# Nine norm statistics as two rounded passes, with the low parts of the squares on VectorE

## The chip, the cores and the metric

The kernel runs on one core of a Trainium2 chip. The metric is the device time of one execution in microseconds (us), as the median of several executions. A profile of one execution of the kernel before is at hand: its span is counted from the first to the last instruction, and all times of the trace are from the start of that span.

## The reference, cut to what matters

The model is a decoder of two layers. Each layer norms its input, projects it to queries, keys and values of three kinds of heads, mixes tokens, projects back, and runs a squared-ReLU MLP. Everything is float32. The change concerns the norms of the sparse-attention (dsa) and latent-attention (mla) queries and keys:

```
y = xf * rsqrt(mean(xf * xf, axis=-1) + RMS_EPS)        # rms_norm

q_d = rms_norm(heads(d_q, 4), dsa_q_norm)               # heads of 64
k_d = rms_norm(heads(d_k, 4), dsa_k_norm)
q_m = heads(rms_norm(m_cq, mla_q_latent_norm) @ mla_w_uq, 4)     # heads of 96
q_m = rms_norm(q_m, mla_q_norm)
k_m = rms_norm(concatenate([k_nope, k_rope]), mla_k_norm)
score = sum over 8 index heads of iw * relu(iq . ik), and the 128 largest keys of each query are kept
```

With 512 tokens, `min(256, L // 4)` keeps 128 keys for each query.

## The kernel before, in words

Activations lie with features on the 128 partitions and the 512 tokens in the free dimension. The mean square of a norm is a sum over partitions, so it is a matmul on TensorE: ScalarE writes the squares into `sqb` (two buffers in turn), TensorE multiplies them by `ones` or by the block matrix `blk`, and every output partition gets the sum. ScalarE then makes the factor from it with Ln and Exp (`factor`, `key_factor`) in `rsb`, and VectorE multiplies by the factor (`dsa_queries`, `dsa_keys`, `mla_queries`, `mla_keys`).

The weights come as a stream of units of 128x1024 floats. ScalarE makes a rounded high part of each unit in `wh` (type float32r), and the low part `wl = raw - wh` is a subtraction: by VectorE for units up to 10 (`low_part`), by GpSimd for later units of the input projection (`POOL_LOW`). A unit of the projection is 24 matmuls on float32r operands: high by low, high by high, low by high, for each of 8 blocks of inputs. The input projection has 24 units (`UNITS`, 0 to 23), in this order around the change: 8, 9 the dsa queries dq0 and dq1; 10, 11 the dsa keys dk0 and dk1; 12, 13 the GLA queries gq0 and gq1; 14, 15 the GLA keys gk0 and gk1; 16 to 19 the gates gg0 to gg3; 20 to 23 the GLA values.

Between the units TensorE runs small float32 matmuls in an order written out by hand: after unit 10 the statistic of mla query head 0 (`mqst0`) and of dq1 (`dqst1`), then the matmul of mla query head 1 (`mla_q(1)`); after unit 11 `mqst1`, `dkst0`, `mla_q(2)`; after unit 12 `mqst2`, `dkst1`, `mla_q(3)`; after unit 13 `mqst3`, the rotation `krot`, `mla_k(0)`; after unit 14 `mkst0` (two matmuls that add up in one bank) and `mla_k(1)`; after unit 15 `mkst1` and `mla_v(0)`.

Every engine has a queue of its own in program order, and they meet at semaphores. For unit u, ScalarE's loop waits for the unit's end, makes the high part of unit u+2 (`split`), and then does `tasks(u)`. VectorE's loop does `evacuations(u)` (it waits for the unit's end and takes the bank out of PSUM), then a number of selection steps (`per_slot`), then its own `tasks(u)`. A selection step finds the next eight largest scores of a block of 128 queries (MAX8) and marks them as taken (MATCH_REPLACE8) over a row of 512, 384 or 256; there are 48 in a layer. GpSimd's loop waits for the high part, makes the low part, and then scales decays (`scale_decay`) and turns queries (`turn_query`). `mla_queries(h)` is two VectorE instructions on operands in SBUF. In `factor`, the Exp of a statistic waits for `nrs_used` of the statistic two places earlier in `NORMS`, because there are two buffers `rsb`:

```python
act.wait_ge(*nrs_used.at(l, i - 2))
act.activation(rsb[0:rows, i % 2, cols], lnb[0:rows, cols], ACT.Exp, scale=-0.5)
```

NORMS runs: cqst, ckvst, dqst0, mqst0, dqst1, mqst1, dkst0, mqst2, dkst1, mqst3, mkst0, mkst1, and then nine of the later stages. So the factor of mqst1 waits until `mla_queries(0)` is done, that of mqst2 for `mla_queries(1)`, and that of mqst3 for `mla_queries(2)`.

Of the kernel before, what the change touches and what calls it, by code (L numbers as in the profile page):

```python
# [15 lines left out]
F32 = mybir.dt.float32  # L16
# [4 lines left out]
P = 128  # L21
T = 512
# [184 lines left out]
ACT_LINKS = 2  # L207


def build_trunk(nc, x_in, stream, params, consts, out):  # L210
    with ExitStack() as ctx:
# [36 lines left out]
        vm, _ = place("vm", [P, TB, H * DH])  # L248
        gated, _ = place("gated", [P, 2, T])
# [27 lines left out]
        ones, _ = place("ones", [P, P])  # L277
        low_rows, _ = place("low_rows", [P, P])
# [72 lines left out]
        nsq_ready = S("nsq_ready", N_NORM)  # L351
        nrs_ready = S("nrs_ready", N_NORM, start=1)
# [83 lines left out]
        def _(pool):  # L436
# [18 lines left out]
            for l in range(DEPTH):  # L455
# [30 lines left out]
                for u in POOL_LOW:  # L486
                    pool.wait_ge(*hi_ready.at(l, u + AHEAD))
                    pool.tensor_tensor(wl[:, u % 2], raw[:, u % 2], wh[:, u % 2], ALU.subtract)\  # L488
                        .then_inc(lo_ready.sem, 1)
                    if u == 9:  # L490
                        pool.wait_ge(const_loaded, 16)
                        scale_decay(0, 0)
                        scale_decay(0, 1)
                        turn_query(0, scaled.at(l, 1))
                    if u in (10, 11):
                        scale_decay(1, u - 10)
                        turn_query(u - 9, scaled.at(l, u - 8))
# [35 lines left out]
        def _(pe):  # L533
# [63 lines left out]
            for l in range(DEPTH):  # L597
# [30 lines left out]
                def mla_q_stat(h):  # L628
                    stat(l, f"mqst{h}", ones[0:QK, 0:QK], sq_of(f"mqst{h}")[0:QK], QK)
# [83 lines left out]
                pe.wait_ge(*rows_ready.at(0, 4))  # L713
# [10 lines left out]
                stat(l, "dqst1", blk, sq_of("dqst1"))  # L724
# [3 lines left out]
                stat(l, "dkst0", blk, sq_of("dkst0"))  # L728
# [3 lines left out]
                stat(l, "dkst1", blk, sq_of("dkst1"))  # L732
# [246 lines left out]
        def _(act):  # L979
# [47 lines left out]
            act.wait_ge(const_loaded, 16)  # L1027
            for l in range(DEPTH):
# [16 lines left out]

                def query_square(h):

                    square(f"mqst{h}", B[f"mq{h}"][0:QK, :], slice(0, QK), wait=B.filled(l, f"mq{h}"))
# [41 lines left out]
                def tasks(u):  # L1090
# [46 lines left out]
                    if u == 9:  # L1137
                        query_square(0)
                        factor("dqst0", DH)
                        square("dqst1", dqr[:, 1], wait=B.freed(l, "dq1"))  # L1140
                    if u == 10:
                        factor("mqst0", QK, QK)
                        query_square(1)
                        factor("dqst1", DH)
                        square("dkst0", dkn[:, 0], wait=B.freed(l, "dk0"))
                    if u == 11:
                        factor("mqst1", QK, QK)
                        query_square(2)
                        factor("dkst0", DH)
                        square("dkst1", dkn[:, 1], wait=B.freed(l, "dk1"))  # L1150
# [146 lines left out]
        def _(vec):  # L1297
# [8 lines left out]
            vec.memset(turn_rows[QK:P], 0.0).then_inc(rows_ready.sem, 1)  # L1306

# [40 lines left out]
            for l in range(DEPTH):  # L1348
# [155 lines left out]
                def tasks(u):  # L1504
# [25 lines left out]
                    if u == 9:  # L1530
                        mla_turn(0)
                        dsa_queries(0)
                    if u == 10:
                        mla_queries(0)
                        mla_turn(1)
                        dsa_queries(1)
                    if u == 11:
                        mla_queries(1)
                        mla_turn(2)
                        dsa_keys(0)  # L1540
                    if u == 12:
                        mla_queries(2)
                        mla_turn(3)
# [347 lines left out]
```

## Time and profile before

| | |
|---|---|
| median of 3 runs | 1248.28 us (1248.27 to 1248.38) |
| the profiled execution | 1248.1 us |
| its span | 1246.3 us, 17707 instructions |
| TensorE (PE) busy | 1236.8 us, 99% of the span |
| VectorE (DVE) busy | 753.1 us, 60% |
| ScalarE (ACT) busy | 527.2 us, 42% |
| GpSimd (POOL) busy | 227.5 us, 18% |
| granted TensorE clock | 1.000 |

Matmuls overlap in the records, so the duration of one is more than the distance from one start to the next; that distance is the price of a matmul in a full row. The shares are means over the whole span, in which the MLP takes by far the longest part; the change lies in a stretch of some 50 us in each of the two layers.

### The profile page before, as it was taken

The numbers are of one execution on the slowest core, as the hardware profiler recorded it, in microseconds if no ns is written. First come the engines' busy times: TensorE is split into PE (matmuls) and PEld (weight loads), VectorE is DVE, ScalarE is ACT, GpSimd is POOL, SyncE is SP. The second block draws the span as 40 slices with busy tenths as digits, with TensorE's granted clock in tenths as the row PEclk, the third lists the DMA queues.
The fourth block names the chain that finished last, engine by engine and source line by source line (L and its number), as shares of the span: only waits on it lengthen the run. The fifth ranks groups of instructions, "written<-read, shape, count | busy, mean of one in ns | idle before, by whom it ended". The sixth has DMA issues, their size and how long they took to land.

```text
span 1246.3 us, 17707 instructions
## 1 busy us (share of the span) xinstructions
PE 1236.8 (99%) x5956; PEld 974.4 (78%) x5956; DVE 753.1 (60%) x1220; ACT 527.2 (42%) x858; POOL 227.5 (18%) x154
## 2 busy tenths in 40 slices
PE   9999999999999999999999999999999999999998
PEld 7766876688888888888886668767888888888887
DVE  6799868644544554544758988585445445445444
ACT  5674448644223224224437643585442242232331
POOL 1044430020120110210520544201201102002002
PEclk9999999999999999999999999999999999999999
DMA  6212220023223323223322222101223233222323
GB/s 247 86 52 67 71 83 2 21 99 131 89 97 101 99 87 101 101 85 101 101 91 79 68 68 85 52 2 52 84 101 101 84 101 101 88 97 101 99 96 109
DMA packets 30721, 108.37 MB, mean 87 GB/s; under 512 B 3536, under 2 KB 3536, under 8 KB 30672
## 3 DMA queue, kind: packets, MB, share of 16 engines
q1 hardware_dynamic: 29520, 103.82, 25.0%
q0 software_dynamic: 432, 2.86, 0.6%
q10 hardware_dynamic: 720, 1.07, 0.3%
q8 instruction: 27, 0.44, 0.1%
q14 instruction: 22, 0.18, 0.0%
HBM read 105.64 MB, written 2.10 MB: 86 GB/s over the span
## 4 chain that ended last, share of the span: by engine, by line
PE 93%; DVE 3%; ACT 2%; issue 1%; DMA 1%; ACTq 0%; DVEq 0%
PE bank L934 19%; PE bank L935 19%; PE bank L933 19%; PE bank L553 7%; PE bank L555 7%; PE bank L554 7%; PE bank L576 2%; PE bank L574 2%; PE bank L575 2%; PE bank L589 2%; PE bank L815 1%; PE bank L827 1%; PE bank L687 1%; PE bank L842 1%; DVE pb L1640 1%
## 5 line engine op out<-in xcount | busy, mean ns | idle before, releaser
L988 ACT ACTIVATE wh<-raw 128x1024 fp32r<-128x1024 f32 x191 | 201.7, 1056 | 375.6 <-PE bank L935 246.5
L1311 DVE TENSOR_TENSOR wl<-raw,wh 128x1024 fp32r<-128x1024 f32 x161 | 247.7, 1539 | 75.9 <-ACT wh L988 75.7
L933 PE MATMUL bank<-hh,wl 128*128 128x512 f32 x512 | 200.0, 391 | 0.0
L933 PE MATMUL bank<-xmh,wl 128*128 128x512 f32 x512 | 199.4, 389 | 0.0
L935 PE MATMUL bank<-hl,wh 128*128 128x512 f32 x512 | 199.2, 389 | 0.0
L935 PE MATMUL bank<-xml,wh 128*128 128x512 f32 x512 | 199.2, 389 | 0.0
L934 PE MATMUL bank<-hh,wh 128*128 128x512 f32 x512 | 199.2, 389 | 0.0
L934 PE MATMUL bank<-xmh,wh 128*128 128x512 f32 x512 | 199.2, 389 | 0.0
L518 POOL TENSOR_TENSOR x<-x,rsb 128x512 f32<-128x512 f32 x62 | 82.0, 1322 | 587.4 <-DVE rsb L1730 587.4
L1719 DVE TENSOR_TENSOR sqb<-tf 128x512 f32<-128x512 f32 x64 | 44.3, 692 | 181.6 <-ACT hh L1274 181.6
L553 PE MATMUL bank<-xgh,wl 128*128 128x512 f32 x368 | 151.1, 411 | 1.2 <-DVE xgl L1324 0.8
L555 PE MATMUL bank<-xgl,wh 128*128 128x512 f32 x368 | 143.6, 390 | 0.0
L554 PE MATMUL bank<-xgh,wh 128*128 128x512 f32 x368 | 143.5, 390 | 0.0
L1272 ACT ACTIVATE tf<-bank 128x512 f32<-128x512 f32 x64 | 38.3, 598 | 204.5 <-PE bank L935 204.5
L1730 DVE TENSOR_TENSOR rsb<-bank,rb 128x512 f32<-128x512 f32 x64 | 44.3, 692 | 128.1 <-PE bank L935 125.9
L933 PEld LDWEIGHTS bank<-hh,wl 128*128 128x128 f32 x512 | 96.1, 188 | 20.4 <-issue 0.5
L934 PEld LDWEIGHTS bank<-hh,wh 128*128 128x128 f32 x512 | 96.1, 188 | 20.4 <-issue 0.5
L933 PEld LDWEIGHTS bank<-xmh,wl 128*128 128x128 f32 x512 | 96.1, 188 | 20.4 <-DVE xml L1324 0.4
L488 POOL TENSOR_TENSOR wl<-raw,wh 128x1024 fp32r<-128x1024 f32 x30 | 72.7, 2425 | 214.6 <-ACT wh L988 214.6
L935 PEld LDWEIGHTS bank<-hl,wh 128*128 128x128 f32 x512 | 96.1, 188 | 19.9
L934 PEld LDWEIGHTS bank<-xmh,wh 128*128 128x128 f32 x512 | 96.1, 188 | 19.9
L935 PEld LDWEIGHTS bank<-xml,wh 128*128 128x128 f32 x512 | 96.1, 188 | 19.9
(218 smaller groups left out, 1663.9 us busy)
## 6 DMA issues: line engine op xcount, KB each, us to landing
raw<-in_stream SPq DMA_DIRECT2D x191, 512.0 KB, 3.2
out_y<-x SPq DMA_DIRECT2D x8, 256.0 KB, 3.7
x<-in_x ACTq DMA_DIRECT2D x4, 256.0 KB, 6.5
x<-in_x SPq DMA_DIRECT2D x4, 256.0 KB, 7.0
con<-in_consts POOLq DMA_DIRECT2D x1, 976.5 KB, 5.1
par<-in_params POOLq DMA_DIRECT2D x1, 916.0 KB, 5.1
par<-in_params POOLq DMA_DIRECT2D x1, 896.0 KB, 6.6
raw<-in_stream SPq DMA_DIRECT2D x2, 256.0 KB, 4.1
```

What stands on the lines that cost most here:

```text
L488: pool.tensor_tensor(wl[:, u % 2], raw[:, u % 2], wh[:, u % 2], ALU.subtract)\
L518: pool.tensor_tensor(x[:, d], x[:, d], rsb[:, d % 2], ALU.add).then_inc(x_ready.sem, 1)
L553: pe.matmul(bank[:], wk_l, act_h[:, k], start=(n == 0), stop=False)
L554: pe.matmul(bank[:], wk_h, act_h[:, k], start=False, stop=False)
L555: m = pe.matmul(bank[:], wk_h, act_l[:, k], start=False, stop=last)
L933: pe.matmul(B.t[s][:], wl[:, s, n_block(k)], src_h[:, k], start=(k == 0), stop=False)
L934: pe.matmul(B.t[s][:], wh[:, s, n_block(k)], src_h[:, k], start=False, stop=False)
L935: m = pe.matmul(B.t[s][:], wh[:, s, n_block(k)], src_l[:, k], start=False, stop=(k == KB - 1))
L988: act.activation(wh[:, s], raw[:, s], ACT.Copy).then_inc(hi_ready.sem, 1)
L1311: vec.tensor_tensor(wl[:, s], raw[:, s], wh[:, s], ALU.subtract).then_inc(lo_ready.sem, 1)
L1719: vec.tensor_tensor(sqb[:, s], tf[:, s], tf[:, s], ALU.mult).then_inc(hid_ready.sem, 1)
L1730: vec.tensor_tensor(rsb[:, s], B.t[s][:], rb[:], ALU.mult).then_inc(dn_freed[s].sem, 1)
```

## The change

Nine statistics of a layer change: mqst0 to mqst3, dqst1, dkst0, dkst1, mkst0 and mkst1. Instead of one float32 matmul on the squares, TensorE runs two matmuls on float32r operands, one on a rounded high part `sqh` of the squares and one on the low part `sql`, adding up in the same bank. ScalarE makes `sqh` with one more instruction behind each square, after a wait for the square. VectorE makes `sql = sqb - sqh`, and TensorE waits for that. `sqh` and `sql` lie where `gated` and `vm` lie, which are filled later. The matrices `ones_r` and `blk_r` are float32r copies, made once at the start.

On VectorE the turn of query head h (`mla_turn`) moves from `tasks` to a place ahead of the selection steps of units 9 to 12, and behind it come the low parts of that unit's two statistics, also ahead of the selection steps. The low part of mkst0 stands at the end of `tasks(13)`, that of mkst1 at the start of `tasks(14)`. The selection steps of units 9 to 13 go from 3 each to 1, 1, 2, 2, 2; later units take more. On GpSimd, `turn_query` comes before `scale_decay`, and the four `scale_decay` move from units 9, 9, 10, 11 to units 10, 10, 11, 12. In mkst0 and mkst1 the matmul on `turn_rows` now comes first.

```diff
+FIRST_PART, N_PARTS = 3, 9
+        sqh, _ = place("sqh", [P, 2, T], F32R, at=gated0)
+        sql, _ = place("sql", [P, 2, T], F32R, at=vm0)
...
-                        scale_decay(0, 0)
-                        scale_decay(0, 1)
-                        turn_query(0, scaled.at(l, 1))
-                    if u in (10, 11):
-                        scale_decay(1, u - 10)
-                        turn_query(u - 9, scaled.at(l, u - 8))
-                    if u == 12:
-                        turn_query(3, lo_ready.at(l, u + AHEAD))
+                    if 9 <= u <= 12:
+                        turn_query(u - 9, lo_ready.at(l, u + AHEAD))
+                    if u == 10:
+                        scale_decay(0, 0)
+                        scale_decay(0, 1)
+                    if u in (11, 12):
+                        scale_decay(1, u - 11)
...
+            def stat_parts(l, name, lhsT, rows=P):
+                i = norm_index(name)
+                pe.wait_ge(*nsl_ready.at(l, i - FIRST_PART))
+                pe.wait_ge(*B.vacant(l, name))
+                pe.matmul(B[name][0:rows, :], lhsT, sqh[0:rows, i % 2], start=True, stop=False)
+                return pe.matmul(B[name][0:rows, :], lhsT, sql[0:rows, i % 2], start=False, stop=True)
...
-                    pe.wait_ge(*nsq_ready.at(l, norm_index(name)))
                     pe.wait_ge(*krsq_ready.at(l, 0))
                     pe.wait_ge(*B.vacant(l, name))
-                    pe.matmul(B[name][:], blk, sq_of(name), start=True, stop=False)
-                    pe.matmul(B[name][:], turn_rows[:], cqn[:, 1], start=False, stop=True)\
+                    pe.matmul(B[name][:], turn_rows[:], cqn[:, 1], start=True, stop=False)
+                    pe.wait_ge(*nsl_ready.at(l, i - FIRST_PART))
+                    pe.matmul(B[name][:], blk_r[:], sqh[:, i % 2], start=False, stop=False)
+                    pe.matmul(B[name][:], blk_r[:], sql[:, i % 2], start=False, stop=True)\
...
+            act.activation(blk_r[:], blk, ACT.Copy).then_inc(blk_ready.sem, 1)
...
+                def square_high(name, src, rows=slice(0, P), wait=None):
+                    i = norm_index(name)
+                    if wait is not None:
+                        act.wait_ge(*wait)
+                    link(act.activation(sqb[rows, i % 2], src, ACT.Square))
+                    act.activation(sqh[rows, i % 2], sqb[rows, i % 2], ACT.Copy).then_inc(nsq_ready.sem, 1)
...
+            vec.memset(ones_r[:].bitcast(F32), 1.0).then_inc(rows_ready.sem, 1)
...
+                def square_low(name, rows=slice(0, P)):
+                    i = norm_index(name)
+                    vec.wait_ge(*nsq_ready.at(l, i))
+                    vec.tensor_tensor(sql[rows, i % 2], sqb[rows, i % 2], sqh[rows, i % 2], ALU.subtract)\
+                        .then_inc(nsl_ready.sem, 1)
...
+                        square_low("mkst0")
                     if u in (14, 15):
                         pr = u - 14
+                        if pr == 0:
+                            square_low("mkst1")
                         mla_keys(pr)
...
-                per_slot = {9: 3, 10: 3, 11: 3, 12: 3, 13: 3, 14: 3, 15: 3, 16: 4, 17: 4, 18: 4,
-                            19: 4, 20: 4, 21: 3, 22: 2}
+                per_slot = {9: 1, 10: 1, 11: 2, 12: 2, 13: 2, 14: 3, 15: 4, 16: 5, 17: 5, 18: 5,
+                            19: 5, 20: 5, 21: 3, 22: 3}
...
                     evacuations(u)
                     if 6 <= u < POOL_LOW[0]:
                         low_part(u % 2, hi_ready.at(l, u + AHEAD))
+                    if 9 <= u <= 12:
+                        mla_turn(u - 9)
+                        square_low(f"mqst{u - 9}", slice(0, QK))
+                    if u == 9:
+                        square_low("dqst1")
+                    if u in (10, 11):
+                        square_low(f"dkst{u - 10}")
                     select_steps(done, per_slot.get(u, 0))
```

The four lines `mla_turn(0)` to `mla_turn(3)` in VectorE's `tasks(9)` to `tasks(12)` go, and each `square` and `stat` of the nine statistics becomes `square_high` and `stat_parts`.

## Rows read from the trace of the kernel before

**Rows 1.** The page: busy time of each engine.
```profile
PE 1236.8 (99%) x5956; PEld 974.4 (78%) x5956; DVE 753.1 (60%) x1220; ACT 527.2 (42%) x858; POOL 227.5 (18%) x154
```

**Rows 2.** Windows: length, each engine's busy us and instructions, units 11 and 12.
```profile
80.87:89.79 8.92, 8.92 (x33) 5.96 (x32) 8.76 (x23) 5.45 (x9) 5.18 (x3) 1.00 0.17 59
89.79:98.72 8.93, 8.93 (x33) 5.97 (x32) 8.76 (x15) 5.16 (x8) 5.14 (x3) 1.00 0.19 61
```

**Rows 3.** Timeline of TensorE: start, us, engine, line, operation, tiles.
```profile
75.64 0.40 PE L554 MATMUL bank<-xgh,wh 128*128 128x512 f32 x1
...
80.64 0.39 PE L555 MATMUL bank<-xgl,wh 128*128 128x512 f32 x1
80.87 1.02 PE L589 MATMUL bank<-sqb,ones 96*96 96x512 f32 x2
81.73 1.02 PE L589 MATMUL bank<-sqb,con 128*128 128x512 f32 x2
```

**Rows 4.** Timeline of ScalarE around units 10 and 11.
```profile
75.61 0.59 ACT L1044 ACTIVATE sqb<-bank 96x512 f32<-96x512 f32 x1 [1.43 <-PE bank L625]
76.11 0.68 ACT L1053 ACTIVATE tf<-bank,par 96x512 f32<-96x512 f32 x1
76.67 0.68 ACT L1061 ACTIVATE lnb<-bank,con 128x512 f32<-128x512 f32 x1
77.38 0.63 ACT L1065 ACTIVATE rsb<-lnb 128x512 f32<-128x512 f32 x1
...
91.66 0.63 ACT L1065 ACTIVATE rsb<-lnb 96x512 f32<-96x512 f32 x1
```

**Rows 5.** Timeline of VectorE, then of GpSimd, units 9 to 12.
```profile
79.92 0.69 DVE L1366 TENSOR_TENSOR dqr<-bank,rb 128x512 f32<-128x512 f32 x1
...
82.64 0.54 DVE L1392 MATCH_REPLACE8 sel<-m,sel 128x384 f32<-128x384 f32 x1
...
89.71 0.69 DVE L1419 TENSOR_TENSOR qT<-tf,rsb 96x512 f32<-96x512 f32 x1
...
91.22 2.87 DVE L1400 SCALAR_TENSOR_TENSOR dqn<-dqr,par,rsb 128x512 f32<-128x512 f32 x1
...
100.04 0.75 DVE L1405 SCALAR_TENSOR_TENSOR dkn<-dkn,par,rsb 128x512 f32<-128x512 f32 x1
...
79.68 1.16 POOL L475 TENSOR_TENSOR tf<-tf,con 32x512 f32<-32x512 f32 x1
82.36 2.36 POOL L488 TENSOR_TENSOR wl<-raw,wh 128x1024 fp32r<-128x1024 f32 x1 [1.52 <-ACT wh L988]
...
91.19 2.35 POOL L488 TENSOR_TENSOR wl<-raw,wh 128x1024 fp32r<-128x1024 f32 x1 [3.57 <-ACT wh L988]
93.50 1.75 POOL L470 TENSOR_TENSOR e<-e,rb 128x512 f32<-128x512 f32 x1
...
100.12 2.91 POOL L488 TENSOR_TENSOR wl<-raw,wh 128x1024 fp32r<-128x1024 f32 x1 [3.70 <-ACT wh L988]
```

**Rows 6.** Timeline in the MLP; then L1311's duration, ns minimum/median/maximum.
```profile
333.37 1.29 POOL L518 TENSOR_TENSOR x<-x,rsb 128x512 f32<-128x512 f32 x1 [1.10 <-DVE rsb L1730]
333.61 2.13 DVE L1311 TENSOR_TENSOR wl<-raw,wh 128x1024 fp32r<-128x1024 f32 x1 [0.32 <-ACT wh L988]
...
L1311 DVE TENSOR_TENSOR wl<-raw,wh x161: 1212/1225/2136, 13.7 to 1232.7; 128x1024 fp32r<-128x1024 f32 x161
```

**Rows 7.** Timeline of VectorE: three selection steps, and unit 13's evacuation.
```profile
80.53 1.47 DVE L1388 MAX8 m<-sel 128x8 f32<-128x512 f32 x3
...
83.60 0.76 DVE L1410 SCALAR_TENSOR_TENSOR qT<-bank,par,con 32x512 f32<-32x512 f32 x1
...
108.35 0.68 DVE L1491 SCALAR_TENSOR_TENSOR gqp<-bank,kinv 64x512 f32<-64x512 f32 x1
```

**Rows 8.** Timeline of VectorE: after the last selection step, and the start.
```profile
173.39 0.29 DVE L1640 CUSTOM_DVE_ANT_0 pb<-bank,con 128x128 f32<-128x128 f32 x1 [9.23 <-PE bank L815]
...
5.35 0.69 DVE L1316 TENSOR_TENSOR wl<-raw,wh 128x512 fp32r<-128x512 f32 x1 [1.70 <-ACT wh L1014]
```

More of the change, by code:

```diff
@@ L206 @@
 VEC_LINKS = 400
-ACT_LINKS = 2
+FIRST_PART, N_PARTS = 3, 9
+ACT_LINKS = 2 + N_PARTS
 def build_trunk(nc, x_in, stream, params, consts, out):
@@ L247, in build_trunk @@
         dkn, _ = place("dkn", [P, 2, T])
-        vm, _ = place("vm", [P, TB, H * DH])
-        gated, _ = place("gated", [P, 2, T])
+        vm, vm0 = place("vm", [P, TB, H * DH])
+        gated, gated0 = place("gated", [P, 2, T])
+        sqh, _ = place("sqh", [P, 2, T], F32R, at=gated0)
+        sql, _ = place("sql", [P, 2, T], F32R, at=vm0)
         xmh, _ = place("xmh", [P, KB, T], F32R, at=m0)
@@ L277, in build_trunk @@
         ones, _ = place("ones", [P, P])
+        ones_r, _ = place("ones_r", [P, P], F32R)
+        blk_r, _ = place("blk_r", [P, P], F32R)
         low_rows, _ = place("low_rows", [P, P])
@@ L351, in build_trunk @@
         nsq_ready = S("nsq_ready", N_NORM)
+        nsl_ready = S("nsl_ready", N_PARTS)
+        blk_ready = S("blk_ready", 0)
         nrs_ready = S("nrs_ready", N_NORM, start=1)
@@ L628, in mla_q_stat @@
                 def mla_q_stat(h):
-                    stat(l, f"mqst{h}", ones[0:QK, 0:QK], sq_of(f"mqst{h}")[0:QK], QK)
+                    pe.wait_ge(*blk_ready.at(0, 0))
+                    stat_parts(l, f"mqst{h}", ones_r[0:QK, 0:QK], QK).then_inc(*B.on_fill(f"mqst{h}"))
                 def mla_k(pr):
@@ L712, in _ @@
                 pe.wait_ge(*B.vacant(l, "cqst"))
-                pe.wait_ge(*rows_ready.at(0, 4))
+                pe.wait_ge(*rows_ready.at(0, 5))
                 pe.matmul(B["cqst"][:], ones[:], sqb[:, 0], start=True, stop=False)
@@ L723, in _ @@
                 mla_q_stat(0)
-                stat(l, "dqst1", blk, sq_of("dqst1"))
+                stat_parts(l, "dqst1", blk_r[:]).then_inc(*B.on_fill("dqst1"))
                 mla_q(1)
@@ L727, in _ @@
                 mla_q_stat(1)
-                stat(l, "dkst0", blk, sq_of("dkst0"))
+                stat_parts(l, "dkst0", blk_r[:]).then_inc(*B.on_fill("dkst0"))
                 mla_q(2)
@@ L731, in _ @@
                 mla_q_stat(2)
-                stat(l, "dkst1", blk, sq_of("dkst1"))
+                stat_parts(l, "dkst1", blk_r[:]).then_inc(*B.on_fill("dkst1"))
                 mla_q(3)
@@ L1044, in square @@
                     act.activation(sqb[rows, norm_index(name) % 2], src, ACT.Square).then_inc(nsq_ready.sem, 1)
+                def square_high(name, src, rows=slice(0, P), wait=None):
[4 more added lines that the diff above has]
+                    act.activation(sqh[rows, i % 2], sqb[rows, i % 2], ACT.Copy).then_inc(nsq_ready.sem, 1)
                 def query_square(h):
-                    square(f"mqst{h}", B[f"mq{h}"][0:QK, :], slice(0, QK), wait=B.filled(l, f"mq{h}"))
+                    square_high(f"mqst{h}", B[f"mq{h}"][0:QK, :], slice(0, QK), wait=B.filled(l, f"mq{h}"))
                     if h == 0:
@@ L1139, in tasks @@
                         factor("dqst0", DH)
-                        square("dqst1", dqr[:, 1], wait=B.freed(l, "dq1"))
+                        square_high("dqst1", dqr[:, 1], wait=B.freed(l, "dq1"))
                     if u == 10:
@@ L1144, in tasks @@
                         factor("dqst1", DH)
-                        square("dkst0", dkn[:, 0], wait=B.freed(l, "dk0"))
+                        square_high("dkst0", dkn[:, 0], wait=B.freed(l, "dk0"))
                     if u == 11:
@@ L1149, in tasks @@
                         factor("dkst0", DH)
-                        square("dkst1", dkn[:, 1], wait=B.freed(l, "dk1"))
+                        square_high("dkst1", dkn[:, 1], wait=B.freed(l, "dk1"))
                     if u == 12:
@@ L1156, in tasks @@
                         factor("mqst3", QK, QK)
-                        square("mkst0", B["mk0"][:], wait=B.filled(l, "mk0"))
+                        square_high("mkst0", B["mk0"][:], wait=B.filled(l, "mk0"))
                     if u == 14:
-                        square("mkst1", B["mk1"][:], wait=B.filled(l, "mk1"))
+                        square_high("mkst1", B["mk1"][:], wait=B.filled(l, "mk1"))
                     if u in (14, 15):
@@ L1396, in use_factor @@
                     return rsb[:, norm_index(name) % 2]
+                def square_low(name, rows=slice(0, P)):
+                    i = norm_index(name)
+                    vec.wait_ge(*nsq_ready.at(l, i))
+                    vec.tensor_tensor(sql[rows, i % 2], sqb[rows, i % 2], sqh[rows, i % 2], ALU.subtract)\
+                        .then_inc(nsl_ready.sem, 1)
                 def dsa_queries(pr):
@@ L1530, in tasks @@
                     if u == 9:
-                        mla_turn(0)
                         dsa_queries(0)
@@ L1534, in tasks @@
                         mla_queries(0)
-                        mla_turn(1)
                         dsa_queries(1)
@@ L1538, in tasks @@
                         mla_queries(1)
-                        mla_turn(2)
                         dsa_keys(0)
@@ L1542, in tasks @@
                         mla_queries(2)
-                        mla_turn(3)
                         dsa_keys(1)
```

## The prediction, made before the changed kernel ran

> **What bounds the kernel now.** I read the page first. TensorE is busy 99% of the span [rows 1], so time is saved only by taking work from TensorE, and lost by making it wait. The next question is whether the engines that get the new work have room in the stretch where it lands; for that I cut the trace into windows at the starts of the statistics. In a mean over the span VectorE is 60% busy, but in the windows of units 11 and 12, each with the small matmuls ahead of it, it is busy 8.76 of 8.92 and 8.76 of 8.93 us [rows 2]: there it is as full as TensorE, which it just keeps up with. Last I read the timelines of all engines through one layer, 72 to 130 us, because what decides is which wait ends last; the rows 3 to 8 are from these.
>
> **What TensorE gains.** From 75.64 to 80.64 lie 22 float32r matmuls: 0.227 us each, 5.46 for a unit. A float32 statistic takes 81.73 - 80.87 = 0.86 [rows 3]. Two float32r passes take 0.455, so each statistic gives back 0.40. Nine of them in two layers: 18 x 0.40 = 7.2 us. Units 11 to 13 then start every 8.1 us instead of 8.9.
>
> **What the others pay, by the row.** ScalarE: one more copy. An instruction of its kind follows 0.50 us after the one ahead (76.11 - 75.61), and one that waits for the one ahead starts 0.03 after its end (76.67 + 0.68, then 77.38) [rows 4]. So the copy starts 0.62 after the square and the next instruction 0.50 after the copy: 0.62 more. ScalarE is busy 5.45 of 8.92 us [rows 2], so this is a delay and no load. The copy writes a rounded value, which no row of 512 here shows on ScalarE; I bound it by the two plain ones, 0.50 and 0.71 from start to start (77.38 - 76.67), and take the first, whose form it has. VectorE: nine subtractions of 0.69 (the 128x512 one at 5.35 us has this type [rows 8]), eight of them by the end of unit 13's tasks: 5.3 us net of overlap. It gives up 7 selection steps there, at 3.07 us for three (83.60 - 80.53 [rows 7]): 7.2 us. By load alone the change fits. The 7 steps go to units 15 to 22. VectorE idles 9.23 us before the attention [rows 8], so they are free there. The memset and the copy at the start lie under a wait of 1.70 us [rows 8], also free. No DMA is added or moved. GpSimd's order costs nothing in itself (it is busy 5.18 of 8.92 us [rows 2]).
>
> **What decides: the two engines exclude each other.** In rows 5, VectorE's `dsa_queries(1)` reads SBUF operands, is issued at 91.22 just behind GpSimd's low part of 91.19, and ends at 94.09, which is 0.55 after GpSimd's end; it costs 0.75 alone. GpSimd's next op runs to 95.25, 1.16 after VectorE's end. At 100.12 GpSimd meets the VectorE op of 100.04, takes 2.91 instead of 2.35, and ends 2.24 after that op [rows 5]. The same holds for a subtraction like the new one: 2.13 us beside GpSimd's 1.29, where 1.225 is its median [rows 6]. In contrast an instruction with one operand in PSUM keeps its 0.69 at 79.92, beside GpSimd's of 79.68, and MATCH_REPLACE8 its 0.54 at 82.64, beside 82.36 [rows 5]; I take `mla_turn` as the former and MAX8 as the latter. So I reckon: a VectorE op with two SBUF inputs, issued during a GpSimd op, ends 0.5 after that op; GpSimd's ends 1.16 (low part: 2.24) after VectorE's; and they alternate. GpSimd's low part runs from 1.4 to 3.8 us after each unit's end (unit end 89.79, low part 91.19, and 2.35 long [rows 2, 5]).
>
> Every `square_low` and both instructions of every `mla_queries` are of this kind. Before, `mla_queries(0)` ended at 90.40, just ahead of the low part. No row shows one of these in collision. The Trainium skill, SBUF — State Buffer, "Who interferes with whom", says that a VectorE instruction with two SBUF inputs contends with a GpSimd instruction that reads SBUF and that whoever issues first holds the port for the whole instruction; it speaks against this change. By it the sum is the one below; if `mla_queries` were free of it, three delays of about 2.2 us would go in each layer and the sum would fall to near 1241 us, the rival of full gain.
>
> **The new schedule, layer 0** (the second repeats it). Until 74 us nothing moves.
> Unit 10 ends at 80.87 as before. q0's square, copy and `tf` end at 77.40 (75.61 + 0.62 + 0.50 + 0.67). VectorE: `mla_turn(0)` 78.7, low of mqst0 by 80.2, dqst1 by 80.8: in time for 80.87 and 81.33. Unit 11 ends 88.98.
> In unit 10: q1 is there at 83.7, `tf` at 85.5, so `mla_turn(1)` ends 86.3 and the low of mqst1 waits for the turn on GpSimd: 87.2. The low of dkst0 waits for `scale_decay(0,0)`: 88.9. In time for 89.44, no stall. One step, then `mla_queries(0)` at 90.05. Its first part ends 90.74, and now the low part (issued 90.38) has its turn until 92.98, so the second part ends 93.48, against 90.40 before.
> The factor of mqst1 waits for that: Exp at 93.5 (before 91.66, after a slack of 1.3 [rows 4, 5]). Behind it on ScalarE stand the square of q2 (to 94.6), its copy, `tf` (95.8), the factor of dkst0 and the square and copy of dkst1 (98.2). VectorE: `mla_turn(2)` 96.6, low of mqst2 behind the turn 97.6, low of dkst1 behind `scale_decay(1,0)` 99.25. TensorE wanted them at 97.09 and 97.55: it goes on with `mla_q(3)` at 99.8 instead of 98.0. Stall 1.8.
> Unit 13 ends at 107.0. `mla_queries(1)` ends 102.9; q3's chain gives `mla_turn(3)` 106.1 and the low of mqst3 at 107.0: stall 0.1. Two steps to 108.8, inside the low part (108.4 to 110.75): `mla_queries(2)` ends 112.0, `dsa_keys(1)` 112.8, the two evacuations of gq1 114.15 (before, they began at 108.35, 4.4 earlier [rows 7]), two steps (2.23) to 116.4. Unit 14 ended at 115.0, the low part runs 116.4 to about 118.7 or 119.3: `mla_queries(3)` ends 119.9. Then krot, the key sum, and the low of mkst0, 0.7 each: 122.1. TensorE wants it after unit 14 and the `turn_rows` matmul, at 115.85. Stall 6.4.
> From there VectorE works on ahead: mkst1's low at 126.5 for 129.9, `mla_keys(1)` frees its bank at 136.2 for 136.5, and five steps with an evacuation (6.0 a unit against TensorE's 5.5 to 6.3) end before the attention needs it. No stall.
>
> **The sum.** Per layer -3.6 + 1.8 + 0.1 + 6.4 = +4.7; two layers +9.4. Span 1246.3 + 9.4 = 1255.7; the profiled execution's own time is 1.8 over its span and the median of the runs 0.2 over that: **1257.6 us**. Bounds of the unknown: the copy between 0.50 and 0.71 moves nothing but the slack; a tie of GpSimd's turn and a VectorE op at 77.55 costs 0.45 per layer if lost (+0.9); the last low part missed in unit 14 (VectorE 1.5 earlier) gives 2.3 back per layer (-4.6). Starting `mla_queries(0)` on time, without the first block, I still reach stalls of 0.6 and 5.6, for the low part returns each unit: +2.6 per layer, 1253.5. With margin for small errors in a chain this long, 1252 to 1260 for this case.
>
> **Rivals.**
> 1. Full gain: VectorE passes each low part. The load sum above speaks for it (7.2 given up, 5.3 taken); the timeline against it: to pass ahead of the first low part, `mla_queries(0)` must start at 89.0 and not 90.05, and likewise in units 12 to 14. From there on: stalls 0, 1246.3 - 7.2 + 2.0 = 1241.1 us.
> 2. Stall equals gain: two of the three low parts are missed, last stall 2.0 (6.4 - 2 x 2.2); per layer -3.6 + 1.8 + 0.1 + 2.0 = +0.3, so 1248.9 us; with one missed 1253.3.
> 3. The lateness goes on: `mla_keys(1)`, only 0.3 ahead of `mla_v(1)`, meets one more GpSimd op of 2.4: 1257.6 + 4.8 = 1262.4 us.
> 4. The change fails to act (a float32r pass on this operand as slow as float32): excluded by rows 3, same shapes.
>
> **How the numbers follow.** A difference of 0.2% (2.5 us) is about what can be told from none. Forecast case 0.60, all slower; rival 1 0.22, faster; rival 2 0.12, 0.11 of it within 0.2% and 0.01 faster; rival 3 0.06, slower. Slower 0.66, same 0.11, faster 0.23. Leaving out rival 1 and 3 would leave out 0.28, so the range reaches down past rival 1, with 1 us for its own error: 1240 to 1260; the forecast's own is 1252 to 1260.
>
> **What would show it.** Right: TensorE waits on VectorE's low part before mkst0, some 6 us in each layer, and about 1 to 2 us before mqst2 and dkst1; statistics 0.23 from start to start; `mla_queries` instructions of 2 to 3 us beside GpSimd's low part; ScalarE's Exp of mqst1 after `mla_queries(0)`. Wrong: the second instruction of `mla_queries(0)` at 0.69 and VectorE's evacuation of gq1 starting within 2 us of unit 13's end; then the time is near 1241.

## The result and the profile after

The changed kernel takes 1263.37 us (median of 4 executions, 1262.60 to 1263.69) against 1248.28 before: 15.1 us slower, ratio 1.0121 [1.0109, 1.0133]. The forecast was 1257.6 us: the sign is right, but the loss is 15.1 us where 9.3 was forecast, and the time lies above the range. The profiled execution takes 1263.69 us, its span is 1261.5, and the mean granted clock is 0.993, where it was 1.000.

The page's busy times, beside [rows 1]:

```profile
PE 1237.0 (98%) x5956; PEld 976.3 (77%) x5956; DVE 775.4 (61%) x1239; ACT 538.6 (43%) x877; POOL 228.0 (18%) x154
```

TensorE is no less busy than before, although 18 statistics got shorter: the slow passes shown below count as busy. The view of TensorE's waits (line waited in, what ended the wait, us in total, times, longest) says where it stood idle; such a time is called a stand below:

```profile
PE bank L660 <- DVE sql L1426: 10.2, 2, 6.1
PE bank L601 <- issue: 2.1, 3, 1.0
PE bank L601 <- DVE sql L1426: 1.9, 2, 1.0
```

L660 is the first rounded pass of mkst0, L601 that of the other statistics. Before, there were no low parts of squares to wait for. TensorE's timeline in the first layer:

```profile
89.61 0.39 PE L601 MATMUL bank<-sqh,ones_r 96*96 96x512 f32 x1
89.84 0.39 PE L602 MATMUL bank<-sql,ones_r 96*96 96x512 f32 x1
90.07 0.40 PE L601 MATMUL bank<-sqh,blk_r 128*128 128x512 f32 x1
...
90.54 1.02 PE L636 MATMUL bank<-cqn,par 128*128 128x512 f32 x2
...
98.73 0.45 PE L601 MATMUL bank<-sqh,ones_r 96*96 96x512 f32 x1 [0.82 <-issue]
...
100.38 0.51 PE L601 MATMUL bank<-sqh,blk_r 128*128 128x512 f32 x1 [0.97 <-DVE sql L1426]
...
116.25 1.02 PE L658 MATMUL bank<-cqn,turn_rows 128*128 128x512 f32 x2
123.42 0.79 PE L660 MATMUL bank<-sqh,blk_r 128*128 128x512 f32 x1 [6.14 <-DVE sql L1426]
124.01 0.63 PE L661 MATMUL bank<-sql,blk_r 128*128 128x512 f32 x1
...
126.57 0.63 PE L560 MATMUL bank<-xgh,wh 128*128 128x512 f32 x1
127.00 0.62 PE L561 MATMUL bank<-xgl,wh 128*128 128x512 f32 x1
```

Two statistics now take 90.54 - 89.61 = 0.93 us, where two took 1.72 at the prices of [rows 3]: the gain of 0.40 each is there in this pair. Then come the stands before mqst2 and dkst1 (0.82 and 0.97) and before mkst0 (6.14). And behind the last one the passes of an ordinary unit follow each other by 127.00 - 126.57 = 0.43 us, where [rows 3] have 0.227: for some us TensorE ran at the lower of its two clock levels, 1.2 and not 2.4 GHz.

What VectorE did meanwhile (its timeline):

```profile
90.93 0.68 DVE L1448 TENSOR_TENSOR tf<-tf,qT 32x512 f32<-32x512 f32 x1
91.65 2.75 DVE L1450 TENSOR_TENSOR qT<-tf,rsb 96x512 f32<-96x512 f32 x1
...
109.89 2.49 DVE L1448 TENSOR_TENSOR tf<-tf,qT 32x512 f32<-32x512 f32 x1
...
113.93 0.68 DVE L1522 SCALAR_TENSOR_TENSOR gqp<-bank,kinv 64x512 f32<-64x512 f32 x1
...
117.71 2.75 DVE L1448 TENSOR_TENSOR tf<-tf,qT 32x512 f32<-32x512 f32 x1
...
122.67 0.69 DVE L1426 TENSOR_TENSOR sql<-sqb,sqh 128x512 fp32r<-128x512 f32 x1
```

and GpSimd beside it:

```profile
90.95 2.91 POOL L495 TENSOR_TENSOR wl<-raw,wh 128x1024 fp32r<-128x1024 f32 x1
...
109.47 2.37 POOL L495 TENSOR_TENSOR wl<-raw,wh 128x1024 fp32r<-128x1024 f32 x1 [0.17 <-ACT wh L1004]
117.58 2.34 POOL L495 TENSOR_TENSOR wl<-raw,wh 128x1024 fp32r<-128x1024 f32 x1 [5.74 <-ACT wh L1004]
```

L1448 and L1450 are the two instructions of `mla_queries`. At 91, 110 and 117 us one of them meets GpSimd's low part and takes 2.5 to 2.75 us instead of 0.7. The second of these puts off the evacuation of gq1 (113.93, where [rows 7] have 108.35), and the third the low part of mkst0, which is VectorE's 122.67 for which TensorE stood from 117.3. ScalarE's timeline shows the other effect, the Exp of mqst1 held by `mla_queries(0)`; in [rows 4] it starts at 91.66:

```profile
90.78 0.67 ACT L1085 ACTIVATE lnb<-bank,con 96x512 f32<-96x512 f32 x1
...
94.50 0.63 ACT L1089 ACTIVATE rsb<-lnb 96x512 f32<-96x512 f32 x1 [3.05 <-DVE qT L1450]
```

Last, two pairs of windows, each of layer 0 and layer 1 (length, busy us and instructions of each engine, granted clock, DMA share, GB/s): from mkst0's first rounded pass to the start of unit 16, and from dkst1's first pass to mqst3:

```profile
123.42:134.25 10.83, 10.83 (x37) 7.82 (x37) 8.84 (x19) 4.60 (x7) 1.74 (x2) 0.81 0.00 0
746.39:758.02 11.63, 11.63 (x37) 8.37 (x37) 8.84 (x19) 4.60 (x7) 1.74 (x2) 0.75 0.11 42
...
100.38:108.26 7.88, 7.88 (x31) 5.60 (x31) 7.27 (x14) 3.94 (x7) 3.95 (x3) 1.00 0.19 68
723.92:733.35 9.43, 9.43 (x30) 6.42 (x31) 8.98 (x19) 3.95 (x7) 5.01 (x3) 0.82 0.15 56
```

The second pair holds the same work, and takes 1.55 us more in layer 1, at a lower clock.

### The profile page after: what moved, and what is told of

Same layout as the page of the kernel before. It is cut to its first block, busy times and chain, and to the rows that moved or that the text cites. A ratio compares the mean times of both kernels' runs of the same rounds, so it can differ in the third digit from the quotient of the medians.

```text
span 1261.5 us, 17745 instructions
## 1 busy us (share of the span) xinstructions
PE 1237.0 (98%) x5956; PEld 976.3 (77%) x5956; DVE 775.4 (61%) x1239; ACT 538.6 (43%) x877; POOL 228.0 (18%) x154
## 4 chain that ended last, share of the span: by engine, by line
PE 86%; DVE 7%; ACT 4%; issue 3%; DMA 1%; ACTq 0%; DVEq 0%
PE bank L951 18%; PE bank L949 18%; PE bank L950 18%; PE bank L559 5%; PE bank L560 5%; PE bank L561 5%; PE bank L582 2%; PE bank L580 2%; PE bank L581 2%; PE bank L831 1%; PE bank L843 1%; PE bank L858 1%; DVE tf L1448 1%; PE bank L595 1%; PE bank L703 1%
```

## The experiments

Each is the changed kernel with one edit, unless said otherwise. The full gain would be 1241.1 us.

### Cause 1: GpSimd's low part

**e1_tiny_low.** GpSimd makes only 8 of the 1024 columns of the low part in units 11 to 17. The rest of these low parts is left out of the computation.

```diff
-    pool.tensor_tensor(wl[:, u % 2], raw[:, u % 2], wh[:, u % 2], ALU.subtract)\
+    part = slice(0, 8 if 9 <= u <= 15 else 1024)
+    pool.tensor_tensor(wl[:, u % 2, part], raw[:, u % 2, part], wh[:, u % 2, part], ALU.subtract)\
```

> The kernel after, with GpSimd's low parts of units 11 to 17 cut to 8 of 1024 columns, so these low parts are left out of the computation; TensorE's work and all waits stay. Theory (VectorE and GpSimd block each other, and the three long blocks by the low part start the lateness): mla_queries instructions all at 0.69 us, no wait of TensorE before mkst0 of more than 1 us, no fall of the clock, 1241 to 1243 us. Rival (VectorE's load and the round over ScalarE are too long by themselves, blocks or none): a wait of 3 us or more before mkst0 stays, 1250 us or more.

Measured: 1248.77 us (1246.89 to 1250.73, 10 runs), 1.0004 [0.9995, 1.0014] of before. Every instruction of `mla_queries` takes 0.68 or 0.69. But TensorE still stands before mkst0, as its waits show:

```profile
PE bank L661 <- DVE sql L1427: 4.4, 2, 2.2
```

So GpSimd's low part accounts for 14.6 of the 22.3 us between the changed kernel and full gain, with the slow passes that its delays bring about. That was less than I expected of it, and the result lies between the two expectations: the other 7.7 us are there with the long collisions gone. 4.4 of them are the waits above, and the clock falls behind the one of layer 0: from 117.34 to 125.84 the passes take 8.50 us at a granted clock of 0.80, 1.6 more than the same work in layer 1 (6.92 at 1.00). Why VectorE is still late this run doesn't show; its own order and the short collisions (`scale_decay`, the turns) are what is left, and the later runs change both.

### Cause 2: the place of mkst0's low part

**e2_keys_first.** The low parts of mkst0 and mkst1 stand ahead of the selection steps of units 13 and 14.

```diff
+    if u == 13:
+        square_low("mkst0")
+    if u == 14:
+        square_low("mkst1")
     select_steps(done, per_slot.get(u, 0))
...
-                        square_low("mkst0")
...
-                        if pr == 0:
-                            square_low("mkst1")
```

> The kernel after, with the low parts of mkst0 and mkst1 moved ahead of the selection steps of units 13 and 14. Theory (the 6 us wait is VectorE's place in its queue, and costs more than itself because TensorE's clock falls behind it): low of mkst0 ends near 116.1 us, the wait before mkst0 goes, no clock fall in layer 0's units 14 and 15; the smaller waits before mqst2 and dkst1 stay; per layer -3.6 + 2.7 = about -1, in all 1246 to 1249 us. Rival (the lateness only moves on, to mkst1 or to mla_v(1)): a new wait of 3 us or more there, 1253 us or more.

Measured: 1257.14 us (1256.68 to 1257.57, 4 runs), 1.0068 [1.0051, 1.0085]. The stand before mkst0 is gone, and TensorE waits for `mla_keys` before the matmul that comes later instead, `mla_v`:

```profile
PE bank L670 <- DVE kT L1458: 7.0, 4, 3.0
```

Moving the late instruction forward gives 6.2 us back and moves the rest of the lateness on, as the rival has it: VectorE is still behind when it comes to `mla_keys`. The longest of these stands, in layer 0, is followed by no slow pass; its window has a clock of 1.00:

```profile
128.64 1.13 PE L670 MATMUL bank<-par,ckvn 128*128 128x256 f32 x4 [3.05 <-DVE kT L1458]
...
128.64:134.88 6.24, 6.24 (x28) 5.19 (x28) 6.07 (x16) 0.60 (x1) 1.06 (x1) 1.00 0.28 87
```

### Cause 3: the granted clock after a stand

**e3_warm.** While TensorE would stand before mkst0 it runs the float32 `turn_rows` matmul 7 times more in layer 0 and 5 times in layer 1. Their results are overwritten; they only keep the engine busy.

```diff
     pe.wait_ge(*B.vacant(l, name))
+    if pr == 0:
+        for _ in range((7, 5)[l]):
+            pe.matmul(B[name][:], turn_rows[:], cqn[:, 1], start=True, stop=True)
     pe.matmul(B[name][:], turn_rows[:], cqn[:, 1], start=True, stop=False)
```

> The kernel after, with 7 (layer 0) and 5 (layer 1) extra float32 matmuls on TensorE at the place where it waits before mkst0, 0.86 us each, to a bank that is written anew behind them. Theory (some 2 us per layer are lost because the clock falls to half after TensorE has stood idle): granted clock stays at 1.00 behind mkst0, unit 15 starts 2 us earlier, 1259 to 1261 us in spite of the extra work. Rival (the slow matmuls behind the wait have another cause): the clock falls all the same, 1263 us or more.

Measured: 1260.67 us (1259.97 to 1260.94, 4 runs), 1.0093 [1.0076, 1.0110]: with 12 float32 matmuls more it is 2.7 us faster than the changed kernel. The windows that answer to the first two shown above:

```profile
124.40:133.59 9.19, 9.19 (x39) 6.78 (x37) 6.93 (x16) 4.60 (x7) 1.07 (x2) 1.00 0.02 5
746.30:755.22 8.92, 8.92 (x37) 6.72 (x37) 8.26 (x18) 4.61 (x7) 1.73 (x2) 1.00 0.00 0
```

Behind mkst0 the clock stays at 1.00, and the stretch is 10.83 - 9.19 = 1.6 us shorter in layer 0 and 11.63 - 8.92 = 2.7 in layer 1. In layer 0 the extra matmuls run on to 124.40, though the low part of mkst0 is ready at 122.93: TensorE comes to them 1.7 us later than in the changed kernel (117.93 against 116.25), because here the clock falls behind dkst1's stand in layer 0 (9.47 us at 0.82 from 100.50 to 109.97) and not in layer 1 (7.93 us at 1.00 from 723.20 to 731.13), the reverse of the changed kernel. So each of the long stands before mkst0 costs its length and, behind it, 1.6 to 2.7 us of slow passes.

### Orders that leave VectorE where it was ahead

**e4_queries_first.** `mla_queries` comes right behind the evacuation of its unit.

```diff
+    if 10 <= u <= 13:
+        mla_queries(u - 10)
     if 9 <= u <= 12:
         mla_turn(u - 9)
...
-    mla_queries(0)
```

and so for heads 1 to 3.

> The kernel after, with mla_queries moved from behind the selection steps to right behind the evacuation in units 10 to 13. Theory (the second instruction of mla_queries(0), blocked by the low part, holds back ScalarE's Exp of mqst1 and so all of unit 11): mla_queries(0) ends before 88 us, the Exp of mqst1 at about 91.5 and not 94.5, the waits before mqst2 and dkst1 under 0.5 us, and a shorter wait before mkst0; 1246 to 1254 us. Rival (the round is bound by VectorE's load and the order inside it does not matter): within 2 us of 1263.

Measured: 1255.93 us (1252.22 to 1260.61, 5 runs), 1.0053 [1.0027, 1.0079]. The three Exp no longer wait for `mla_queries`. But now the low parts of the squares stand where `scale_decay` runs on GpSimd; VectorE's timeline, with two of them in one row:

```profile
88.93 2.57 DVE L1426 TENSOR_TENSOR sql<-sqb,sqh 96x512 fp32r<-96x512 f32 x2
```

and TensorE's waits:

```profile
PE bank L601 <- issue: 4.9, 4, 1.6
PE bank L601 <- DVE sql L1426: 3.0, 2, 2.0
```

**e5_both_first.** Both moves, the four `scale_decay` one to each of units 9 to 12, and the selection steps of units 9 to 13 at one each, with more of them later (the sum stays).

```diff
-    per_slot = {9: 1, 10: 1, 11: 2, 12: 2, 13: 2, 14: 3, 15: 4, 16: 5, ..., 20: 5, 21: 3, 22: 3}
+    per_slot = {9: 1, 10: 1, 11: 1, 12: 1, 13: 1, 14: 2, 15: 3, 16: 5, ..., 20: 6, 21: 5, 22: 5}
```

> All nine statistics rounded, with the order mended: mla_queries right behind the evacuation, the low parts of mkst0 and mkst1 ahead of the selection steps, one scale_decay per unit from unit 9 to 12, and five more selection steps moved from units 12 to 15 to units 20 to 22. Theory (order and blocks, not load, cost the time): waits under 1 us each, 1243 to 1247 us. Rival (VectorE has no room for nine low parts anywhere between unit 9 and the attention, where it idled 9.2 us less 3.6 that TensorE gives up): over 1248 us, with new waits on VectorE at mla_v or at the first logits.

Measured: 1252.39 us (1251.54 to 1258.82, 7 runs), 1.0041 [1.0026, 1.0057]. That is closer, but above what I expected, and TensorE still waits: 3.9 us in the statistics and 3.8 for `mla_keys` before `mla_v`.

### Fewer statistics

**e6_three.** Only dqst1, dkst0 and dkst1 are in two passes; `mla_turn` is back in `tasks`, the low part stands behind one selection step, and units 9 to 15 have 2, 2, 2, 3, 3, 3, 3 steps. **e7_five.** The same with mkst0 and mkst1 too, their low parts behind three steps.

```diff
+    PARTS = ['dqst1', 'dkst0', 'dkst1']            # e7_five: and 'mkst0', 'mkst1'
...
+    if name not in PARTS:                          # as the kernel before
...
+        return pe.matmul(B[name][0:rows, :], plain, sqb[0:rows, i % 2], start=True, stop=True)
```

> Three of the nine statistics rounded (dqst1, dkst0, dkst1), whose squares are ready early; mla_turn back in tasks, each low part behind one selection step, GpSimd's order as after, one step less in units 9 to 11. Theory (each rounded statistic gives back 0.40 us where its low part has slack): 3 x 0.40 x 2 = 2.4 us less than before, 1246 us. Rival (any low part in these units costs more through blocks than it gives): 1249 us or more.

> As the kernel with three, and mkst0 and mkst1 rounded too, low parts behind the three selection steps of units 13 and 14. Theory: 5 x 0.40 x 2 = 4.0 us less than before, 1244.3 us. Rival (VectorE, now at 7.85 of 8.34 us busy in unit 14's window, is late there): a wait of TensorE before mkst0 or mv1, 1247 us or more.

Measured: e6_three 1250.56 us (1250.22 to 1250.78, 10 runs), 1.0018 [1.0008, 1.0027]; e7_five 1258.91 (1257.98 to 1259.26, 4 runs), 1.0087 [1.0070, 1.0104]. Three statistics save at most 6 x 0.40 = 2.4 us, and e6_three is still 2.3 us slower than before; TensorE waits 3.0 us in it for `mla_keys` before `mla_v`. VectorE's timeline in it, at the end of unit 14:

```profile
116.80 2.81 DVE L1466 TENSOR_TENSOR qT<-tf,rsb 96x512 f32<-96x512 f32 x1
```

and GpSimd's:

```profile
116.70 2.37 POOL L496 TENSOR_TENSOR wl<-raw,wh 128x1024 fp32r<-128x1024 f32 x1 [5.70 <-ACT wh L1015]
```

VectorE's instruction is issued 0.10 us behind GpSimd's and loses 2.1 us. Both kernels came out above the theory. In e7_five the same befalls the low part of mkst1 (2.62 us at 125.03), and TensorE waits 7.1 us for such low parts. The number of rounded statistics does not order these times: with five in this order the kernel is slower than with nine in that of e5_both_first.

### The GpSimd order alone

**e8_pool_order.** The kernel before, with nothing but the changed order on GpSimd (`turn_query` ahead of `scale_decay`, and these a unit later).

```diff
-    scale_decay(0, 0)
-    scale_decay(0, 1)
-    turn_query(0, scaled.at(l, 1))
+    if 9 <= u <= 12:
+        turn_query(u - 9, lo_ready.at(l, u + AHEAD))
+    if u == 10:
+        scale_decay(0, 0)
+        scale_decay(0, 1)
```

> The kernel before with one part of the change alone, GpSimd's new order (turn_query first, the four scale_decay in units 10, 10, 11, 12). Theory (the order costs TensorE nothing by itself, it only decides which VectorE instruction is blocked): within 0.5 us of before. Rival (this order alone brings VectorE behind by unit 11): 1250 us or more, with the Exp of mqst1 or a bank late.

Measured: 1248.74 us (1248.43 to 1249.03, 10 runs), 1.0003 [0.9994, 1.0013]: no effect that can be told from none.

### All nine, in another order

**e9_nine_ordered.** All nine statistics in two passes. In units 10 to 12 VectorE does: the evacuation, two selection steps, `dsa_queries` or `dsa_keys`, `mla_queries(u - 10)`, `mla_turn`, and the low parts of squares (two in units 10 and 11, one in unit 12); unit 13 has the same without turn and low part. The low parts of mkst0 and mkst1 stay where the changed kernel has them. So the selection steps, which GpSimd doesn't hold up, lie where its low part runs, and the instructions with two SBUF operands lie behind it. One `scale_decay` runs in each of units 10 to 13.

```diff
     evacuations(u)
-    if 9 <= u <= 12:
-        mla_turn(u - 9)
-        square_low(f"mqst{u - 9}", slice(0, QK))
...
     select_steps(done, per_slot.get(u, 0))         # then tasks(u), in place of its old calls:
+    if u in (10, 11):
+        dsa_queries(u - 10)
+    if u in (12, 13):
+        dsa_keys(u - 12)
+    if 10 <= u <= 13:
+        mla_queries(u - 10)
+    if 9 <= u <= 12:
+        mla_turn(u - 9)
+        square_low(f"mqst{u - 9}", slice(0, QK))
+    if u == 9:
+        square_low("dqst1")
+    if u in (10, 11):
+        square_low(f"dkst{u - 10}")
...
+    per_slot = {9: 0, 10: 2, 11: 2, 12: 2, 13: 2, 14: 2, 15: 3, 16: 5, ..., 20: 5, 21: 4, 22: 4}
```

> All nine statistics rounded, with VectorE's order set by when GpSimd holds the port: in units 10 to 15 the evacuation and two or three selection steps come first (they are not blocked, and fill the time of GpSimd's low part), then dsa_queries or dsa_keys, mla_queries, mla_turn and the two low parts; the four scale_decay one in each of units 10 to 13. Theory (the place of the SBUF-only instructions against the low part is the cause, and VectorE has the time): no mla_queries instruction over 1.8 us, the Exp of mqst1 to mqst3 not late, waits of TensorE under 1 us each and no fall of its clock, 1241 to 1244 us. Rival (VectorE is simply full): waits of 2 us or more at the low parts or at mla_v, 1248 us or more.

Measured: 1243.86 us (1243.35 to 1244.53, 6 runs), 0.9966 [0.9954, 0.9979] of before: 4.4 us faster than the kernel before and 19.5 faster than the changed one, with the same instructions in another order. VectorE's timeline from the small matmuls ahead of unit 11:

```profile
82.00 1.15 DVE L1412 MAX8 m<-sel 128x8 f32<-128x512 f32 x2
...
83.12 0.68 DVE L1416 MATCH_REPLACE8 sel<-m,sel 128x512 f32<-128x512 f32 x1
...
84.24 1.29 DVE L1430 SCALAR_TENSOR_TENSOR dqn<-dqr,par,rsb 128x512 f32<-128x512 f32 x1
85.56 0.68 DVE L1447 TENSOR_TENSOR tf<-tf,qT 32x512 f32<-32x512 f32 x1
86.28 1.46 DVE L1449 TENSOR_TENSOR qT<-tf,rsb 96x512 f32<-96x512 f32 x1
87.77 0.76 DVE L1440 SCALAR_TENSOR_TENSOR qT<-bank,par,con 32x512 f32<-32x512 f32 x1
88.56 1.48 DVE L1425 TENSOR_TENSOR sql<-sqb,sqh 96x512 fp32r<-96x512 f32 x2
```

GpSimd's in the same stretch:

```profile
82.59 2.38 POOL L495 TENSOR_TENSOR wl<-raw,wh 128x1024 fp32r<-128x1024 f32 x1 [3.28 <-ACT wh L1003]
86.01 1.18 POOL L482 TENSOR_TENSOR tf<-tf,con 32x512 f32<-32x512 f32 x1 [1.03 <-ACT tf L1076]
```

The low part of 82.59 to 84.97 lies beside MAX8 and MATCH_REPLACE8, which keep their time (1.15 for the two MAX8 and 0.68 for a MATCH_REPLACE8 of 128x512, as at 115.35 and 116.48 in the changed kernel, where GpSimd stood idle); only `dsa_queries(0)`, issued 0.73 before its end, is held, and ends 0.56 after it. The longest `mla_queries` instruction is 1.5 us, and it meets GpSimd's short turn. The windows of units 11 and 12 (same columns as above), beside 8.92 and 8.93 in [rows 2]:

```profile
81.19:89.54 8.35, 8.30 (x33) 5.83 (x32) 8.03 (x14) 6.44 (x11) 5.19 (x3) 1.00 0.19 63
89.54:97.86 8.32, 8.32 (x33) 5.95 (x33) 7.80 (x14) 6.41 (x10) 5.41 (x3) 1.00 0.20 66
```

The view of TensorE's waits has no low part of squares in it, and the clock is 1.00.

**e10_after_decays.** e9_nine_ordered with the `scale_decay` of the changed kernel (units 10, 10, 11, 12). **e11_after_slots.** e9_nine_ordered with the selection steps of the changed kernel.

```diff
-    if u in (10, 11):                              # e10_after_decays
-        scale_decay(0, u - 10)
-    if u in (12, 13):
-        scale_decay(1, u - 12)
+    if u == 10:
+        scale_decay(0, 0)
+        scale_decay(0, 1)
+    if u in (11, 12):
+        scale_decay(1, u - 11)
...
-    per_slot = {9: 0, 10: 2, 11: 2, 12: 2, 13: 2, 14: 2, 15: 3, 16: 5, ..., 21: 4, 22: 4}
+    per_slot = {9: 1, 10: 1, 11: 2, 12: 2, 13: 2, 14: 3, 15: 4, 16: 5, ..., 21: 3, 22: 3}    # e11_after_slots
```

> The ordered kernel with GpSimd's scale_decay put back to where the changed kernel has them (units 10, 10, 11, 12). Theory (VectorE's order carries the gain; GpSimd's short operations cost one block of about 1 us each): within 1 to 2.5 us above the ordered kernel, 1244.5 to 1246.5 us, with a longer wait before dkst0 alone. Rival (the spread decays carry it): 1250 us or more.

> The ordered kernel with the selection steps per unit of the changed kernel (1, 1, 2, 2, 2, 3, 4 in units 9 to 15, against 0, 2, 2, 2, 2, 2, 3). Theory (order, not the number of steps): one more step in units 14 and 15 may delay mla_v(1), else nothing; 1244 to 1247 us. Rival (it was the count of steps ahead of the attention's units): 1250 us or more.

Measured: e10_after_decays 1244.44 us (1244.40 to 1244.82, 8 runs), 0.9972 [0.9961, 0.9982]; e11_after_slots 1248.38 (1245.21 to 1252.51, 10 runs), 1.0005 [0.9991, 1.0019]. In this order GpSimd's is worth 0.6 us or nothing, so VectorE's order and steps carry the gain. With the changed kernel's steps the new order still gives 15.0 us back, but not the last 4.5. The runs of e11_after_slots fall into two groups of five, 1245.2 to 1246.8 and 1250.0 to 1252.5, so its median stands for neither; the first lies in the expected range, the second in the rival's. The mean granted clock is 0.998 to 1.000 in the first group and 0.996 to 0.998 in the second, which speaks for stands or slow passes there; only a run of the first was profiled, so which ones stays open. The new steps with the old order were not run.

## Why the prediction was too low

**What the profile bears out.** In layer 0 the places of the waits, and nearly all of their lengths. "Stall 1.8" before mqst2 and dkst1: 0.82 + 0.97 = 1.79. "Stall 6.4" before mkst0: 6.14. `mla_queries(0)` was to end at 93.48 and ended at 94.40, the Exp of mqst1 was to start at 93.5 and starts at 94.50, the evacuation of gq1 was to end at 114.15 and ended at 115.31 (its second instruction starts 0.69 behind the one at 113.93, and takes 0.69). The forecast's rule for two engines that exclude each other carries this: instructions of 96x512 and 32x512 with two SBUF operands, of which no row of before showed a collision, take 2.5 to 2.8 us beside GpSimd's low part, as the one of 128x512 in [rows 5] did; by the Trainium skill, SBUF — State Buffer, "Who interferes with whom", they were to do so, and the trace agrees. e1_tiny_low shows that this is the larger cause: 14.6 us. The selection steps, taken to be free of it by one row of MATCH_REPLACE8, are free of it, which e9_nine_ordered lives on.

**The step that failed** is "The sum. Per layer -3.6 + 1.8 + 0.1 + 6.4 = +4.7". It lacks a term: each stand of TensorE was priced at its length alone, as if the passes behind it would run at 0.227 us. The forecast has 115.85 + 6.4 = 122.25 for mkst0's first rounded pass and 126.43 + 4.7 = 131.13 for the start of unit 16, 8.9 us between them. The trace has 10.83 in layer 0 at a granted clock of 0.81, and 11.63 in layer 1 at 0.75: 2.0 and 2.7 us more. By e3_warm, in which the clock holds, 1.6 and 2.7 of it is the clock; e9_nine_ordered has 8.92 for the same 37 passes at 1.00 (115.24 to 124.16). From the start of unit 10 to that of unit 16 layer 0 loses 7.8 us and layer 1 7.6, where 4.7 each was forecast: the slow passes behind mkst0's stands are 4.7 of the 6.0 us that are missing. The rest is 1.2 us in layer 0 and 0.2 in layer 1 ahead of mkst0's pass. Every row of before has a clock of 1.00, since TensorE stood nowhere in this stretch; the forecast didn't ask what happens to it when TensorE stands 6 us.

**The second term** is smaller: "a tie of GpSimd's turn and a VectorE op at 77.55 costs 0.45 per layer if lost (+0.9)" was taken as won. It is lost in layer 0 and won in layer 1, by the same distance of 0.05 us; VectorE's and GpSimd's rows, of both layers:

```profile
77.55 1.42 DVE L1470 SCALAR_TENSOR_TENSOR sel<-rel_last,iws,sel 128x256 f32<-128x256 f32 x1
77.60 1.09 POOL L482 TENSOR_TENSOR tf<-tf,con 32x512 f32<-32x512 f32 x1 [0.89 <-ACT tf L1077]
...
701.54 0.48 DVE L1470 SCALAR_TENSOR_TENSOR sel<-rel_last,iws,sel 128x256 f32<-128x256 f32 x1
701.59 1.38 POOL L482 TENSOR_TENSOR tf<-tf,con 32x512 f32<-32x512 f32 x1 [0.89 <-ACT tf L1077]
```

In layer 0 VectorE's instruction is the one held up (1.42 for 0.48), in layer 1 GpSimd's (1.38 for 1.09). So unit 11 ends at 89.61 in layer 0 where 88.98 was forecast, 0.63 late, and in layer 1 it ends 13.99 us behind the start of unit 10, where the forecast has 13.97. The matmul of query head 3, which starts at 100.96 for the forecast's 99.8, is 1.2 late: `mla_queries(0)` had begun and ended 0.9 late.

**Layer 1 is not the repeat** that "The second repeats it" makes of it. The clock falls behind dkst1's stand (9.43 us against 7.88 in layer 0), so TensorE comes to mkst0's wait 2.5 us later than forecast, and stands 4.05 us there for the forecast's 6.4. `mla_queries(3)` passes ahead of GpSimd's low part, one of the forecast's bounds ("gives 2.3 back per layer"), but the key sum behind it is held instead (1.98 us at 743.63). That mkst0's pass still comes within 0.2 us of the forecast is luck: the path to it was another.

**The bound of the other side.** "Starting `mla_queries(0)` on time, without the first block, I still reach stalls of 0.6 and 5.6, for the low part returns each unit" treats the block as bound to come back. It is not: in e4_queries_first the Exp no longer wait for `mla_queries`, and in e9_nine_ordered all nine statistics fit. The load sum of the forecast ("By load alone the change fits") is right; no run reaches rival 1's time. Even e9_nine_ordered reaches 4.4 of the 7.2 us: up to the start of unit 16 its layer 0 gains 2.6 of 3.6 (124.16 - 75.33 = 48.8 us from the start of unit 10, where before took 126.43 - 75.01 = 51.4). Of the last 1.0, 0.3 is missing in the small matmuls ahead of unit 15 (2.08 us, where before took 2.18 and 1.78 was due), 0.2 in those ahead of unit 12 (2.45 for 2.24), and 0.2 in unit 11's matmuls (6.11 us, and 5.89 before). Why these are longer isn't settled.

## What to carry to other kernels

Before an instruction with two SBUF operands is added to VectorE, draw up where GpSimd's long instructions run in each unit, and fill those places with work that GpSimd doesn't hold up (here the selection steps, or operands in PSUM); the same nine statistics cost 15 us in one order and gave 4 in another. When a predicted wait makes TensorE stand for several us, ask what slow passes follow it, and give the sum a bound for them (here 0 behind a stand of 3.05 us, and 1.6 to 2.7 behind 4 and 6 us). And an engine that is full in the windows where the work lands must be followed past the first late instruction: moving that one forward alone (e2_keys_first) only moved the wait.

## What the runs showed of the hardware

- Stands of 6.14 and 4.05 us were followed by passes at 0.43 us from start to start instead of 0.227, and by granted clocks of 0.81 and 0.75 over the next 11 us. 0.43 and 0.227 are TensorE's levels of 1.2 and 2.4 GHz. The Trainium skill, TensorE: Matmul & The Clock Gate, "What's actually happening", says that the lower level is the default and that activity releases it; this trace agrees in so far as the passes behind these two stands came back to 0.227 us while TensorE went on working.
- A shorter stand may do it or not. After the waits that end at 98.73 and 100.38 in layer 0 no pass is slow; after the same two waits in layer 1, at 722.28 and 723.92 (1.01 and 0.97 us), the stretch from the second statistic's low pass to the next unit takes 2.52 us instead of 1.55, and that up to mqst3 1.55 more. In e3_warm it is layer 0 that slows and layer 1 that doesn't. Stands of 3.05 us (e2_keys_first) and 1.86 us (e3_warm, layer 1) left the clock at 1.00, and of two of 2.2 us in e1_tiny_low one was followed by slow passes. What decides this the rows don't show. TensorE's timeline of layer 1:

```profile
722.28 0.44 PE L601 MATMUL bank<-sqh,ones_r 96*96 96x512 f32 x1 [1.01 <-issue]
...
723.92 0.50 PE L601 MATMUL bank<-sqh,blk_r 128*128 128x512 f32 x1 [0.97 <-DVE sql L1426]
724.27 0.39 PE L602 MATMUL bank<-sql,blk_r 128*128 128x512 f32 x1
...
726.79 1.42 PE L559 MATMUL bank<-xgh,wl 128*128 128x512 f32 x1
```

- A VectorE instruction issued 0.10 us behind GpSimd's low part took 2.81 us instead of 0.69 (e6_three), and a MATCH_REPLACE8 beside such a low part took its usual 0.68 (e9_nine_ordered, at 83.12).
- When the two are issued 0.05 us apart, the recorded order doesn't tell who is held up: in layer 0 it was the VectorE instruction (1.42 us for 0.48), in layer 1 GpSimd's (1.38 for 1.09), and the traces of e2_keys_first to e5_both_first repeat this, layer by layer.
